# Row tables ahead of the gated products, row buffers cleared in the odd layer, token-major norm statistics, in a 256-token three-layer transformer kernel

## What is computed

```python
def rms_norm(x, gain):                       # six times with scale and shift, once plain at the end
    y = xf * rsqrt(mean(xf * xf, axis=-1) + EPS)
    return y * gain

# first block: norm, projections, attention and pooling, output, norm, conv feed-forward
h = rms_norm(x, norm1_g) * (1 + scale1) + shift1
...
x = x + gate1 * (merged @ w_out)
h2 = rms_norm(x, norm2_g) * (1 + scale2) + shift2
u = causal_dwconv(h2 @ w_up, conv_w, conv_b)
x = x + gate2 * ((silu(u_g) * u_v) @ w_down)
# even layer: norm, two kinds of attention, norm, gated feed-forward (silu(h@g) * (h@u)) @ d
# odd layer:  norm, attention over the best 256 keys, norm, then
#   8 experts, each (silu(h@g_e) * (h@u_e)) @ d_e for the tokens whose router picked it (2 of 8)
x = rms_norm(x, final_norm)
```

## Time and profile before

| | us |
|---|---|
| median of 3 runs | 1455.48 (1452.39 to 1460.26) |
| the profiled execution | 1466.41, span of its instructions 1464.8 |
| TensorE busy | 1361.5 (93% of the span) |
| VectorE busy | 451.0 (31%) |
| ScalarE busy | 271.7 (19%) |
| granted TensorE clock, mean | 0.968 of full |

### The profile page before, as it was taken

How to read it: one execution, slowest core, us unless ns; L and a number is a source line. 1 busy time by engine, 2 the same in 40 slices (tenths; PEclk the granted TensorE clock), 3 DMA queues, 4 the chain that set the end, 5 groups by cost and what they waited for, 6 DMA issues and landing times.

```text
span 1464.8 us, 24958 instructions
## 1 busy us (share of the span) xinstructions
PE 1361.5 (93%) x10058; PEld 984.7 (67%) x10058; DVE 451.0 (31%) x1199; ACT 271.7 (19%) x667; POOL 71.2 (5%) x127
## 2 busy tenths in 40 slices
PE   4999999899999898999999989988949999999997
PEld 2758787788888666778888867766524455444535
DVE  7225352443455125132323334542140000000003
ACT  3332203112112325220000021253100010000002
POOL 1001010000000000000000000000010000000010
PEclk8999999999999999999999999999979999999999
DMA  9988689767676531346666830006995999999991
GB/s 360 402 331 336 229 310 341 261 250 266 242 293 243 174 126 58 99 145 260 243 265 237 339 106 14 1 11 238 357 367 189 369 389 349 352 377 371 333 349 39
DMA packets 91916, 367.15 MB, mean 251 GB/s; under 512 B 10385, under 2 KB 10513, under 8 KB 83336
## 3 DMA queue, kind: packets, MB, share of 16 engines
q1 hardware_dynamic: 75008, 271.81, 51.4%
q0 software_dynamic: 16848, 94.52, 17.3%
HBM read 347.28 MB, written 19.01 MB: 250 GB/s over the span
## 4 chain that ended last, share of the span: by engine, by line
PE 82%; SPq 5%; DVE 5%; DMA 2%; issue 2%; ACT 2%; another core or an unknown queue 1%; DVEq 0%; ACTq 0%; POOLq 0%
PE banks L583 20%; PE banks L770 20%; PE banks L752 10%; PE banks L1017 9%; PE banks L1069 6%; PE banks L608 4%; SPq L479 3%; PE banks L1040 3%; SPq L486 2%; PE banks L638 1%; DMA ring<-experts 1%; PE banks L621 1%; DMA ring<-stream 1%; PE banks L694 1%
## 5 line engine op out<-in xcount | busy, mean ns | idle before, releaser
L770 PE MATMUL banks<-h,ring 128*128 128x256 f32 x1408 | 314.7, 382 | 4.0 <-ACT h L1159 4.0
L770 PEld LDWEIGHTS banks<-h,ring 128*128 128x128 f32 x1408 | 270.1, 192 | 42.3 <-issue 4.9
L583 PE MATMUL banks<-h,ring 128*128 128x256 f32 x832 | 189.0, 386 | 9.8 <-ACT h L1159 8.7
L583 PEld LDWEIGHTS banks<-h,ring 128*128 128x128 f32 x832 | 158.0, 192 | 40.0 <-issue 13.5
L1017 PE MATMUL banks<-ring,arena 128*32 128x512 f32 x1536 | 174.3, 593 | 4.6 <-DMA ring<-experts 4.0
L752 PE MATMUL banks<-arena,ring 128*128 128x256 f32 x704 | 162.1, 383 | 4.8 <-DVE arena L1541 4.8
L1416 DVE CUSTOM_DVE_ANT_0 side<-side 128x1024 f32<-128x1024 f32 x128 | 151.2, 1221 | 34.7 <-DMA side<-ada 34.5
L752 PEld LDWEIGHTS banks<-arena,ring 128*128 128x128 f32 x704 | 134.1, 191 | 25.1 <-DVE arena L1541 5.2
L1017 PEld LDWEIGHTS banks<-ring,arena 128*32 128x32 f32 x1536 | 51.6, 110 | 122.3 <-issue 105.8
L583 PE MATMUL banks<-arena,ring 128*128 128x256 f32 x512 | 114.0, 380 | 2.9 <-ACT arena L1197 1.5
L583 PEld LDWEIGHTS banks<-arena,ring 128*128 128x128 f32 x512 | 97.0, 190 | 17.0 <-ACT arena L1197 2.2
(11 more groups left out here) (263 smaller groups left out, 1011.4 us busy)
## 6 DMA issues: line engine op xcount, KB each, us to landing
ring<-stream SPq DMA_DIRECT2D x247, 512.0 KB, 5.9
ring<-experts SPq DMA_DIRECT2D x192, 512.0 KB, 15.3
side<-ada POOLq DMA_DIRECT2D x64, 1024.0 KB, 7.1
side<-experts SPq DMA_DIRECT2D x48, 512.0 KB, 18.9
arena<-tails SPq DMA_DIRECT2D x32, 384.0 KB, 21.9
hrows<-logit POOLq DMA_DIRECT2D x1, 5376.0 KB, 36.3
yrows<-logit POOLq DMA_DIRECT2D x1, 5376.0 KB, 59.5
logit<-hrows POOLq DMA_DIRECT2D x8, 384.0 KB
```

The costliest lines, as they stand in the source:

```text
L583: last = pe.matmul(bank(u, a, a + T), ring[:, s, (k0 + kc) * P:(k0 + kc + 1) * P], moving[:, kc, :], start=(kc == 0), stop=(kc == kn - 1))
L770: last = pe.matmul(banks[:, b, r * T:(r + 1) * T], ring[:, s, kc * P:(kc + 1) * P], h[:, kc, :], start=(kc == 0), stop=(kc == KC - 1))
```

## The change

Three edits, none of which alters what is computed.

1. **Order in pass 0.** VectorE's `extra_passes`, `row_numbers` and `last_choice` stand ahead of the six gated products instead of behind them. POOL no longer waits for the last pick transpose (`s_picktr`) before it reads the rows of pass 1.
2. **Clearing the row buffers.** POOL clears and writes them after all ada loads, once norm 4 is done (`s_h` 40), from a tile in `side`; VectorE's wait for it ahead of the even layer's attention goes, and SP waits for it before it loads the first expert slot in `side`.
3. **Norm statistics token-major** in norms 1 to 6. For each chunk TensorE holds 128x128 of the squares as weights, twice (one for each 128 tokens), and moves one column of ones, so that the sums are 128x2, one for each token. Root and reciprocal are taken of 128x2. `norm_spread`, two products of 128 columns with the reciprocals broadcast as weights and the identity moving, puts them back on all partitions, and VectorE reads them from the bank. The statistics of norms 1, 3 and 5 go to bank 2 instead of 7, `out_open` waits for nothing and stands ahead of `norm_spread`, and the bank is released after the scale and shift, by a nop.

```diff
@@ -222,6 +222,7 @@
...
         rstd = var[:, T:2 * T]
+        stat2, inv2 = var[:, 0:2], var[:, 4:6]
         logit = sb("logit", [P, KEPT, TRI])
@@ -306,17 +307,17 @@
...
         hgtok = spare[0:CAP, 1280:1280 + D]
-        nought = spare[0:CAP, 0:D]
+        nought = side[0:CAP, 0, :]
         target, origin = spare[:, 496:500].bitcast(I32), spare[:, 500:504].bitcast(I32)
...
         slot_full = [sem(f"slot_full{s}") for s in range(MSLOTS)]
-        slot_used = [sem(f"slot_used{s}") for s in range(MSLOTS)]
+        slot_used = [sem(f"slot_used{s}") for s in range(MSLOTS - 1)]
         ada_full = [sem(f"ada_full{s}") for s in range(2)]
         cond_in = [sem(f"cond_in{n}") for n in range(2)]
-        x_in, cols_in, mats_in, pos_in, onehot_in = (sem(n) for n in ("x_in", "cols_in", "mats_in", "pos_in", "onehot_in"))
+        x_in, cols_in, mats_in, onehot_in = (sem(n) for n in ("x_in", "cols_in", "mats_in", "onehot_in"))
         t5_stored, bias_in, pool_in, sel_in, out_stored = (sem(n) for n in ("t5_stored", "bias_in", "pool_in", "sel_in", "out_stored"))
@@ -366,7 +368,7 @@
...
                 return u.bank, u.done, taken(u)
-            return (0 if r == 6 else 7), (s_sum, (r + 2) // 2), (s_root, (r + 2) // 2)
+            return (0 if r == 6 else 2), (s_sum, (r + 2) // 2), (s_root, (r + 2) // 2)
@@ -469,6 +471,7 @@
...
                     sp.wait_ge(s_mod, 9)
+                    sp.wait_ge(nought_out, 32)
                 elif m == TAIL:
@@ -522,13 +525,6 @@
...
                 ada_load(v)
-            pool.wait_ge(s_pv, 8)
-            pool.memset(nought, 0.0).then_inc(consts_set, 1)
-            pool.wait_ge(consts_set, 4)
-            pool.dma_start(hrows.rearrange("e r n -> r e n"),
-                           nought.rearrange("p (o n) -> p o n", o=1).broadcast_to([CAP, NTAB, D])).then_inc(nought_out, 16)
-            pool.dma_start(yrows.rearrange("e t s q n -> (t s) e (q n)"),
-                           nought.rearrange("p (o n) -> p o n", o=1).broadcast_to([CAP, NTAB, D])).then_inc(nought_out, 16)
             for n in range(2):
@@ -537,6 +533,12 @@
...
+            pool.wait_ge(s_mod, 9)
+            pool.wait_ge(s_h, 40)
+            pool.memset(nought, 0.0).then_inc(consts_set, 1)
+            pool.wait_ge(consts_set, 4)
+            for rows in (hrows.rearrange("e r n -> r e n"), yrows.rearrange("e t s q n -> (t s) e (q n)")):
+                pool.dma_start(rows, nought.rearrange("p (o n) -> p o n", o=1).broadcast_to([CAP, NTAB, D])).then_inc(nought_out, 16)
             pool.wait_ge(nought_out, 32)
@@ -546,7 +548,6 @@
...
             pool.wait_ge(rows_stored, 64)
-            pool.wait_ge(s_picktr, 2)
             pool.dma_start(hgtok, hrows[1]).then_inc(rows_in, 16)
@@ -635,15 +636,32 @@
...
                 pe.wait_ge(s_sq, 8 * r + order.index(c) + 1)
-                ins = pe.matmul(banks[:, norm_bank(r)[0], 0:T], ones[:, :], h[:, c, :], start=(c == order[0]), stop=(c == order[-1]))
+                b = norm_bank(r)[0]
+                if r == 0:
+                    ins = pe.matmul(banks[:, b, 0:T], ones[:, :], h[:, c, :], start=(c == order[0]), stop=(c == order[-1]))
+                else:
+                    for tile in range(2):
+                        ins = pe.matmul(banks[:, b, T + tile:T + tile + 1], h[:, c, tile * P:(tile + 1) * P], ones[:, 0:1],
+                                        start=(c == order[0] and tile == 0), stop=(c == order[-1]), skip_group_check=True)
                 if c == order[-1]:
                     ins.then_inc(norm_bank(r)[1][0], 1)
+
+            def norm_spread(r):
+
+                pe.wait_ge(s_rstd, r + 1)
+                b = norm_bank(r)[0]
+                for tile in range(2):
+                    ins = pe.matmul(banks[:, b, tile * P:(tile + 1) * P], inv2[:, tile:tile + 1].broadcast_to([P, P]), ident,
+                                    start=(tile == 0), stop=(tile == 1), skip_group_check=True)
+                ins.then_inc(s_spread, 1)
...
                     norm_chunk(r, c)
+                if r:
+                    norm_spread(r)
@@ -739,8 +757,8 @@
...
                 u0 = U[name]
-                pe.wait_ge(*norm_bank(r0)[2])
                 out_open()
+                norm_spread(r0)
@@ -944,6 +962,7 @@
...
+            norm_spread(5)
             few_outputs("router", 5)
@@ -1148,7 +1167,10 @@
...
                 act.wait_ge(*done)
-                act.activation(var[:, 0:T], banks[:, b, 0:T], ACT.Sqrt, scale=1.0 / D, bias=eps[:, :]).then_inc(read[0], 1)
+                if r == 0:
+                    act.activation(var[:, 0:T], banks[:, b, 0:T], ACT.Sqrt, scale=1.0 / D, bias=eps[:, :]).then_inc(read[0], 1)
+                else:
+                    act.activation(stat2, banks[:, b, T:T + 2], ACT.Sqrt, scale=1.0 / D, bias=eps[:, :]).then_inc(s_std, 1)
@@ -1158,6 +1180,8 @@
...
                                    bias=mod[:, third, at + c:at + c + 1]).then_inc(s_h, 1)
+                if r:
+                    act.nop().then_inc(norm_bank(r)[2][0], 1)
@@ -1401,14 +1425,19 @@
...
             def norm_root(r):
-                b, done, read = norm_bank(r)
-                dve.wait_ge(*read)
-                dve.reciprocal(rstd, var[:, 0:T]).then_inc(s_rstd, 1)
-                dve.wait_ge(s_rstd, r + 1)
+                if r == 0:
+                    dve.wait_ge(*norm_bank(r)[2])
+                    dve.reciprocal(rstd, var[:, 0:T]).then_inc(s_rstd, 1)
+                    dve.wait_ge(s_rstd, r + 1)
+                else:
+                    dve.wait_ge(s_std, r)
+                    dve.reciprocal(inv2, stat2).then_inc(s_rstd, 1)
+                    dve.wait_ge(s_spread, r)
             def norm_chunks(r, c0, c1):
+                spread = banks[:, norm_bank(r)[0], 0:T] if r else rstd
                 for c in range(c0, c1):
-                    ins = dve.tensor_tensor(h[:, c, :], x[:, c, :], rstd, ALU.mult)
+                    ins = dve.tensor_tensor(h[:, c, :], x[:, c, :], spread, ALU.mult)
                     ins.then_inc(s_xn, 1)
@@ -1656,7 +1684,6 @@
...
                .then_inc(freed[u.bank], 1)
-            dve.wait_ge(nought_out, 32)
             between = {c + 1: [lambda c=c: rope(c, sqT[:, c, :], ("sq", c))] for c in range(4)}
@@ -1864,12 +1891,12 @@
...
-                hidden(0, 0, WIDE)
-                hidden(1, WIDE, NARROW)
                 if first:
...
                     last_choice()
+                hidden(0, 0, WIDE)
+                hidden(1, WIDE, NARROW)
                 dve.wait_ge(s_hidtr, 3 * p + 2)
```

More of the change, by code:

```diff
@@ L326, in program @@
         s_sq, s_sum, s_root, s_rstd, s_xn, s_h = (sem(n) for n in ("s_sq", "s_sum", "s_root", "s_rstd", "s_xn", "s_h"))
+        s_std, s_spread = sem("s_std"), sem("s_spread")
         s_qksq, s_qkrstd, s_qk = sem("s_qksq"), sem("s_qkrstd"), sem("s_qk")
@@ L429, in _ @@
             sp.dma_start(cols[:, :], cols_d).then_inc(cols_in, 16)
-            sp.dma_start(posi, pos_d).then_inc(pos_in, 16)
+            sp.dma_start(posi, pos_d).then_inc(cols_in, 16)
             sp.dma_start(cond[:, 0, :], cond_d[0:1, :].broadcast_to([P, D])).then_inc(cond_in[0], 16)
@@ L1557, in ffn @@
                 norm_vector(2 * third0 // 3 + 1)
-            dve.wait_ge(pos_in, 16)
-            dve.wait_ge(cols_in, 16)
+            dve.wait_ge(cols_in, 32)
             chain = [0]
```

## The result

| | before | after |
|---|---|---|
| median, us | 1455.19 (1452.39 to 1460.26, 4 runs) | 1441.89 (1431.03 to 1448.36, 4 runs) |
| profiled execution, us | 1466.41 (span 1464.8) | 1448.36 (span 1446.8) |
| TensorE busy, us | 1361.5 | 1371.7 |
| granted clock, mean | 0.968 | 0.974 |

The ratio is 0.9896, 95% interval 0.9855 to 0.9938: faster by 1.0%, 13.3 us, where 32 were forecast. The four runs of after lie 17 us apart, and the profiled one is the slowest. Between the two profiled executions 18.0 us were gained.

A forecast was written before the change was run, and what follows sets the result against it. Bound: TensorE's waits and lowered clock, with transfers setting the end after pass 0. Clearing 6.5, norms 1 to 4 4.6, norm 6 1.3 and idle transfers 20.3 sum to 32.7 us: 1466.4 to 1433.7, less 0.75% gives 1423; range 1411 to 1438.

The forecast's parts named there:

- Tables first: Pass 0: two TensorE waits and lowered clock go, 24 us on TensorE's path; 20.3 us of idle transfer time counted.
- 0.75% above the median: Base of the forecast: the profiled execution's excess over three runs' median, taken off as the same share, 1433.7 to 1423.
- set by how soon the transfers are through: After pass 0: transfers, not TensorE's own work, set the end; DMA share 1.03 from 1128 to 1427 us.
- The rows of the last pass: Profile rows before: the last pass's chain runs through a 17.25 us wait on expert weights.
- Net 1.3 us: Norms 2, 4, 5 and 6: saving per norm behind the last sum, after adding 0.73 us for `norm_spread`.
- count nothing: Norm chunk sums: one-column products cost the same as before, with 0.1 us a chunk either way as bounds.
- Rows or slots late: Rival, 13 in 100: pass 1 rows or pass 2 slots come late; 20 to 26 us gained, 1430 to 1436.
- the clock stays up: Rival, 10 in 100: shorter gaps keep TensorE's clock up behind the norms, some 5 us more, 1418.
- The clearing and its 6.5 us: First feed-forward: moving the clearing removes a 4.8 us TensorE stall and 1.7 us of lowered clock.
- The two waits and the lowered clock of pass 0: Pass 0: 12.3 us for `last_choice`, 8.7 for pass 1's rows and 2.9 of lowered clock go, 24 us.
- More wait on ring<-experts than before: Expected sign in the profile after: a little more wait for expert weights in the last passes.
- TensorE-bound: Rival, 12 in 100: TensorE's path, not transfers, sets the end; 37.7 us gained, 1418.

The follow-up runs named there:

- tables_alone: Kernel before with only the pass 0 order changed (row numbers and last choice ahead of the gated products): 1442.69 us, ratio 0.9931.
- tails_full: Changed kernel with the four tail slots of each pass loaded with other data on 128 partitions instead of 96, output wrong: 1417.19 us, ratio 0.9715.
- norms_alone: Kernel before with only the token-major norm statistics added: 1456.87 us, ratio 1.0001.
- before_padded: Kernel before with tail slots padded by zeros from 96 to 128 partitions, nothing else: 1452.12 us, ratio 0.9942.
- padded: Changed kernel with tail slots padded by 32 rows of zeros to 128 partitions, computation unchanged: 1417.13 us, ratio 0.971.
- padded_wide: Changed kernel with tails zero-padded to 128 partitions and norm sums moving 128 columns of ones instead of one: 1410.78 us, ratio 0.966.
- padded_no_norms: Changed kernel with tails zero-padded to 128 partitions but the norm statistics of before: 1424.24 us, ratio 0.975.
- tails_112: Changed kernel with tail slots zero-padded to 112 partitions instead of 128: 1440.48 us, ratio 0.989.
- sides_96: Changed kernel with tails zero-padded to 128 partitions, but four side slots of each later pass loaded on 96, output wrong: 1430.56 us, ratio 0.9847.
- tails_between: Changed kernel with the four 96-partition tail transfers of passes 1 to 7 issued between the side slots: 1457.54 us, ratio 1.0009.

## Why the prediction was wrong

**The step that failed** is in *Tables first*: "Their work isn't changed, so they can only gain their idle time ... I take the whole idle time as regained", 20.3 us. In tables_alone it was 10 to 13. The work in bytes is unchanged; its time is not. In before, the tails of pass 1 were issued at 1102 us, into the half-idle window of 1092 to 1128 us, and their low rate held nothing up there. In after they stand in the full stretch and add their 4.5 us of dip. Between the profiled executions the stretch gave 13.8 us, and 4.5 of the missing 6.5 are that dip; the other 2 I can't assign. With 128 partitions in the tails the changed kernel is 24.7 us faster, the kernel before 6.7: some 18 us of what the change won on TensorE's path went into the slow transfers.

**The base was wrong as well.** The profiled execution of before was "0.75% above the median", and I took that share off the forecast. Its excess was not spread evenly: 5.3 us in pass 6 and 7.1 behind the start of pass 7 (72.6 us to the end, 65.5 in tails_full) went into waits for weights, most of which a typical execution doesn't have (norms_alone's trace; before_padded 1452). I read "set by how soon the transfers are through" from a full share, but in that window TensorE still began every pass up to the sixth on its own pace. I subtracted a gain on the transfers from an end that, in the median run, TensorE's path set, with some 7 to 8 us lost to transfers (before_padded). The rows of the last pass were true, but of one execution.

**The norms.** Forecast were 5.9 us that reach the end; norms_alone gave none. "Net 1.3 us" for each link holds only where the clock does: 1.0 us in norm 6 of padded, 0.9 in norms 2, 4 and 6 of padded_wide, 0.8 in norm 1 (1.0 forecast), but 0.4 and 0.5 in norms 2 and 4 of padded. What failed is "count nothing" for the sums: they take the same time (3.73 us for the sums of a norm at full clock, 3.72 before), but with one column moving the clock falls sooner. I had it as a sub-case of "Rows or slots late", 1 us each, and as the argument against the rival "the clock stays up"; that argument was right. With wide sums the kernel is 13.5 us under padded_no_norms, so that rival's gain is there to be had. In front of the transfers' stretch 4.7 us were gained, 11.1 forecast. Norm 4 took 1.6 us longer than before where 1.3 less was forecast (7.61 us from first sum to first product, 6.05 before). About 4 us more went in the even layer's attention, where after stood 14 us at 0.50 and before 3. That second place doesn't hang on the norms: tables_alone and before_padded stood 14 us at 0.50 there as well, and padded, with the code of after up to pass 0, stood 7. It varies between executions, and the profiled one of before was lucky there.

**The rest.** The clearing and its 6.5 us: right (6.3 alone). The two waits and the lowered clock of pass 0: right, 20 to 24 us for 24. No wait on the two writes: right; they landed by 922 us. More wait on ring<-experts than before: right. The rival "TensorE-bound", 37.7 us, was refuted for this kernel, and is what the kernel becomes with padded tails: 35.0 us. One reading was loose: the ada load of 54.2 us stood behind the writes in POOL's own queue, so it doesn't show transfers of SP and of POOL getting in each other's way.

**The best version** is padded_wide, 1410.78 us: 31 us under the changed kernel, 48 under before beside it (1458.78).

## What to carry to other kernels

Where transfers set the end, read their rate in short windows beside their share, and ask of each dip what alone is in flight there: here the engines were fully busy at little more than half the rate. Where rows of 4 KB go to 96 or 112 partitions in such a stretch, try padding to 128 even at the price of more bytes, and when a stall goes, ask which slow transfers it had covered. Before a wait of the last stage, or a stretch of lowered clock, enters a sum, look whether a second execution has it.

## What the runs showed of the hardware

- Transfers of 4 KB rows to 96 or 112 partitions run at 223 to 290 GB/s with all engines busy (after, tails_112, sides_96), 128 partitions at 408; mixed among wide ones they slow those too (tails_between, 15.6 us).
- They also make the time vary: 17 us between executions of the changed kernel and 18 in tails_112, under 2 in padded. It isn't the only cause: padded_wide and padded_no_norms spread over 8 us.
- TensorE's granted clock fell during an unbroken run of one-column products (norm 4 of after), or right behind it (norms 2 and 4 of padded). The Trainium skill ("TensorE: Matmul & The Clock Gate", section "HAM oscillation — how this bites in real kernels") blames gaps between bursts. In norm 4 of after there was none, and 128 columns instead of one brought the median clock from 0.974 to 0.9845.
- The same code can stand 3 or 14 us at 0.50 in the same attention stage (before, tables_alone), worth some 4 us.
